# The last turn of a gated layer's second down product: two weight pieces taken row block by row block, and two weight splits moved among the norm's blocks

## The chip, the cores and the metric

The kernel runs on one core of a Trainium2 chip. The metric is the device time of one execution in microseconds (us). The time before is 3171.87 us, the median of 3 runs (3171.06 to 3172.69). Engines are named as in the profile: PE (TensorE, matrix products; PEld its weight loads), DVE (VectorE), ACT (ScalarE), POOL (GpSimd) and SP (SyncE, which issues most DMAs).

## The reference, cut to what matters

The program computes two networks one after the other on 512 tokens of width 1024: first two layers with a gated convolutional feed-forward block, then two layers of another kind. All is float32. The change touches only the feed-forward blocks of the first two layers, and what follows each directly.

```python
D_MODEL = 1024; SEQ = 512; D_FF = 2816
def _conv_ffn(u, w_up, conv_w, conv_b, w_down):
    h = _causal_dwconv(u @ w_up, conv_w, conv_b)
    a, g = jnp.split(h, 2, axis=-1)
    return (jax.nn.gelu(g, approximate=False) * a) @ w_down

    # in first_block, for layer i of 2
        u = x * (1.0 + sc2) + sh2
        y = _conv_ffn(u, f_w_up[i], f_conv_w[i], f_conv_b[i], f_w_down[i])
        x = _layer_norm(DEEPNORM_ALPHA * x + (1.0 + g2) * y, ln_g[i, 1], ln_b[i, 1])
```

After layer 0 comes the attention mixer of layer 1 (`u @ w_in`, in the kernel `d_qk` and `d_v`). After layer 1 comes the second network: an RMS norm, a modulation, and the RWKV time mix, whose first products are small low-rank ones (`sigmoid(xg @ g1)`, `tanh(xw @ w1)`, `xa @ a1`) and then `xr @ wr`.

## The kernel before

**Products in split precision.** Each float32 weight tile is split into a high part (ACT, `act_split`, a copy to a rounded type, `w_high`) and a low part (DVE, `dve_split`, the difference, `w_low`). The left or right operand is split likewise (`u_high`, `u_low`). One product is three PE matmuls (`product`): high by high, high by low, low by high.

**Linears, turns and pieces.** A `Linear` is done in turns of 512 output columns. A turn of a "t" linear fills four PSUM banks, one for each block t of 128 tokens (TT is 4). Its weight comes in pieces of some 128-row steps. `f0_dn1` and `f1_dn1`, the second halves of the two layers' down products, have 10 steps in four pieces of 2, 3, 2 and 3 steps, and two turns. In this text pieces are counted from 0, so the last two are pieces 2 and 3. With four row blocks and three matmuls a piece of 2 steps is 24 matmuls and a piece of 3 steps is 36.

**The ring.** Weight tiles of all linears are numbered through and go through a ring of three slots (`SLOTS`). SP loads tile w once PE has used tile w-3, ACT and DVE split it two tiles ahead of PE (`AHEAD`). So in the last turn of `f0_dn1` the splits that ACT and DVE do "ahead" of pieces 0 and 1 are those of pieces 2 and 3, and those ahead of pieces 2 and 3 are of the next linear's first two tiles. These two are called **next0** and **next1** here. They are tiles of 128 x 2048 elements (1 MB). After `f0_dn1` the next linear is `d_qk`, after `f1_dn1` it is `r_r`. next0 takes the slot of piece 1, next1 that of piece 2, and the tile after them that of piece 3.

**Order.** There is no scheduler. The order on each engine is that in which its program is written, and every engine works strictly in that order. In the last turn `act_residual` does three splits (pieces 2 and 3, next0), then the norm step `follow(0)`, then the split of next1, then `follow(1)` to `follow(3)`. `dve_residual` does the split of piece 2, a block of the modulation (`dve_ada`), the splits of piece 3 and of next0 (all by `dve_ahead_all`), then for each row block t a **block** of the residual and norm, and after all four the split of next1. A block begins with `stage<-bank` (the sum times its gate), then the addition to x, the statistics, and in layer 0 the small operations of `dve_ln_behind`, in layer 1 the longer ones of `dve_r_behind` (two of 128 x 1024). On ACT, `follow(t)` takes a square root, then the normalisation of row block t-1 (and of t too, when t is 3). That row block then goes to PE for transposes (`pe_turn_late`), whose results ACT reads out of PSUM (`act_turn`; after layer 1 the first loop of `act_rwkv`) and DVE works on (`dve_turn`; after layer 1 `dve_rwkv`).

SP's order behind next1 is, after layer 0, two modulation tiles of 1 MB (`ada_ring`) and the next weight tile; after layer 1 the three low-rank weights and two more weight tiles.

Of the kernel before, what the change touches and what calls it, by code (L numbers as in the profile page):

```python
# [14 lines left out]
P = 128  # L15
# [3 lines left out]
TT = S // P  # L19
# [14 lines left out]
DECAY = math.exp(-0.5)  # L34
ROWS = 640
SLOTS = 3
AHEAD = 2
D_UNITS = 32
X_UNITS = 64
# [190 lines left out]
class Net:  # L230
# [499 lines left out]
    def pe_linear_t(self, pe, name, x, ends, u=None, hidden=None, between=None, beside=None):  # L730
        L = self.lin[name]
        for i in range(L.turns):
            for q, (k0, nk) in enumerate(L.pieces):
                w = L.tile(i, q)
                final = q == len(L.pieces) - 1
                if beside and final and i == L.turns - 1:
                    beside()
# [20 lines left out]
                self.pe_ada(pe, L.ada[i])  # L758
            if between and i == 0:
                between()  # L760

    def pe_ada(self, pe, b):
        bank = self.ada_bank.get(b, 7)
# [97 lines left out]
    def dve_residual(self, v, name, st, gates, alpha, lnst=None, follow=None):  # L861
        L = self.lin[name]
        v.wait_ge(self.gates_in, st)
        for i in range(L.turns):
            self.dve_ahead_all(v, name, i)
            for t in range(TT):
                xs, tmp = self.X[:, t, i * 512:(i + 1) * 512], self.stage[:, t % 2, :]
                if t == TT - 1 and i < len(L.ada):
                    self.dve_ada_take(v, L.ada[i])
                v.wait_ge(self.T, "sum", name, i, t)  # L870
                v.wait_ge(self.V)
                v.tensor_tensor(tmp, self.sums(name, i, t)[:], gates[:, i * 512:(i + 1) * 512], ALU.mult).then_inc(
                    *self.V.up("got", name, i, t))
                v.wait_ge(self.V)
                if alpha == 1.0:
                    v.tensor_tensor(xs, xs, tmp, ALU.add).then_inc(*self.V.up("x", name, i, t))
                else:
                    v.scalar_tensor_tensor(xs, xs, alpha, tmp, ALU.mult, ALU.add).then_inc(*self.V.up("x", name, i, t))
                if lnst is not None:
                    v.wait_ge(self.V)  # L880
                    v.bn_stats(lnst[:, t, i * 6:(i + 1) * 6], xs).then_inc(*self.V.up())
                if follow and i == L.turns - 1:
                    follow(t)
            self.dve_ahead(v, name, i, len(L.pieces) - 1)

    def act_residual(self, a, name, follow=None, first=None):
        L = self.lin[name]
        for i in range(L.turns):
            self.act_ahead_all(a, name, i)
            late = follow and i == L.turns - 1  # L890
            if not late:
                self.act_ahead(a, name, i, len(L.pieces) - 1)
            for t in range(TT):
                if first and i == 0:
                    first(t)
                if late:
                    follow(t)
                    if t == 0:
                        self.act_ahead(a, name, i, len(L.pieces) - 1)


# [2200 lines left out]
```

## Time and profile before

| what | value |
|---|---|
| time, median of 3 runs | 3171.87 us |
| profiled execution, its own time | 3168.98 us |
| its span | 3167.70 us |
| PE busy | 2987.9 us, 94% |
| PE weight loads busy | 2433.8 us, 77% |
| DVE busy | 2023.9 us, 64% |
| ACT busy | 1096.4 us, 35% |
| POOL busy | 91.1 us, 3% |
| mean granted PE clock | 0.977 |

The times are taken from one profiled execution and counted from the start of its span; the execution lasted 1.28 us more than the span. PE is busy for nearly all of the span, so what matters is where PE stands still. Two such places, around 748 to 760 us and 1443 to 1468 us, follow the two products that the change touches. A "granted clock" of 1.00 is 2.4 GHz and of 0.50 is 1.2 GHz.

### The profile page before, as it was taken

The numbers are of one execution on the slowest core, as the hardware profiler recorded it, in microseconds if no ns is written. First come the engines' busy times: TensorE is split into PE (matmuls) and PEld (weight loads), VectorE is DVE, ScalarE is ACT, GpSimd is POOL, SyncE is SP. The second block draws the span as 40 slices with busy tenths as digits, with TensorE's granted clock in tenths as the row PEclk, the third lists the DMA queues.
The fourth block names the chain that finished last, engine by engine and source line by source line (L and its number), as shares of the span: only waits on it lengthen the run. The fifth ranks groups of instructions, "written<-read, shape, count | busy, mean of one in ns | idle before, by whom it ended". The sixth has DMA issues, their size and how long they took to land.

```text
span 3167.7 us, 45905 instructions
## 1 busy us (share of the span) xinstructions
PE 2987.9 (94%) x19656; PEld 2433.8 (77%) x19656; DVE 2023.9 (64%) x3115; ACT 1096.4 (35%) x1675; POOL 91.1 (3%) x100
## 2 busy tenths in 40 slices
PE   6998999999988999997999988899999999899999
PEld 5876788887866788884868777678888777778887
DVE  5856897787577896887357888654444255554353
ACT  2334432233155432323333333342223344542122
POOL 0000000000000000000002221000000001000000
PEclk8999999999999999998999999899999999999999
DMA  8751554545620554541310000333323220032232
GB/s 240 182 160 56 184 173 163 182 161 171 201 94 26 174 183 143 205 160 55 108 39 9 12 13 10 103 88 105 93 93 95 80 93 27 8 107 93 94 106 80
DMA packets 236543, 346.08 MB, mean 109 GB/s; under 512 B 19620, under 2 KB 121964, under 8 KB 236340
## 3 DMA queue, kind: packets, MB, share of 16 engines
q1 hardware_dynamic: 221236, 329.63, 32.4%
q10 hardware_dynamic: 15104, 13.52, 1.4%
q8 instruction: 154, 2.52, 0.3%
q14 instruction: 49, 0.40, 0.0%
HBM read 340.97 MB, written 2.15 MB: 108 GB/s over the span
## 4 chain that ended last, share of the span: by engine, by line
PE 79%; DVE 13%; ACT 4%; DMA 2%; issue 1%; SPq 0%; DVEq 0%; ACTq 0%
PE bank L141 77%; DVE w_tiles_b L150 2%; PE bank L144 2%; DVE w_tiles L150 1%; DVE w_low L150 1%; DMA first_ada<-in_w_ada 1%; ACT w_high L147 1%; DVE ada_acc L162 1%; DMA weight_ring<-in_d_w_in 1%; DVE w_g L150 1%; DVE x_natural L162 1%; DVE d_sm L168 0%; ACT stage L147 0%; DVE x_sm L168 0%; DVE x_natural L150 0%
## 5 line engine op out<-in xcount | busy, mean ns | idle before, releaser
L150 DVE TENSOR_TENSOR w_low<-weight_ring,w_high 128x2048 fp32r<-128x2048 f32 (+2 forms) x212 | 463.7, 2187 | 449.3 <-ACT w_high L147 449.3
L147 ACT ACTIVATE w_high<-weight_ring 128x2048 fp32r<-128x2048 f32 (+2 forms) x212 | 388.1, 1831 | 606.6 <-DMA weight_ring<-in_mlp_down 177.7
L141 PE MATMUL bank<-u_high,w_high 128*128 128x512 f32 x1472 | 577.2, 392 | 12.6 <-ACT u_high L147 6.4
L141 PE MATMUL bank<-u_high,w_low 128*128 128x512 f32 x1472 | 573.9, 390 | 0.0
L141 PE MATMUL bank<-u_low,w_high 128*128 128x512 f32 x1472 | 573.5, 390 | 0.0
L141 PE MATMUL bank<-w_high,u_high 128*128 128x512 f32 x896 | 353.5, 395 | 6.2 <-DVE w_low L150 2.5
L141 PE MATMUL bank<-w_high,u_low 128*128 128x512 f32 x896 | 351.4, 392 | 0.0
L141 PE MATMUL bank<-w_low,u_high 128*128 128x512 f32 x896 | 351.2, 392 | 0.0
L141 PEld LDWEIGHTS bank<-u_high,w_high 128*128 128x128 f32 x1472 | 276.9, 188 | 70.8 <-ACT stage L147 7.5
L141 PEld LDWEIGHTS bank<-u_high,w_low 128*128 128x128 f32 x1472 | 276.7, 188 | 58.5
L141 PEld LDWEIGHTS bank<-u_low,w_high 128*128 128x128 f32 x1472 | 277.0, 188 | 56.7
L162 DVE SCALAR_TENSOR_TENSOR ada_acc<-ada_ring,silu_c,ada_acc 128x512 f32<-128x512 f32 x336 | 252.6, 752 | 15.7 <-DVE ada_acc L162 0.5
L141 PEld LDWEIGHTS bank<-w_high,u_high 128*128 128x128 f32 x896 | 170.1, 190 | 45.0 <-DVE w_low L150 2.9
L141 PE MATMUL bank<-w_high,g_hidden_low 128*128 128x512 f32 x512 | 199.2, 389 | 0.0
L141 PE MATMUL bank<-w_high,g_hidden_high 128*128 128x512 f32 x512 | 199.2, 389 | 0.0
L141 PE MATMUL bank<-w_low,g_hidden_high 128*128 128x512 f32 x512 | 199.2, 389 | 0.0
L141 PEld LDWEIGHTS bank<-w_high,u_low 128*128 128x128 f32 x896 | 169.6, 189 | 36.0
L141 PEld LDWEIGHTS bank<-w_low,u_high 128*128 128x128 f32 x896 | 169.9, 190 | 35.1
L150 DVE TENSOR_TENSOR g_relu<-g_relu 128x512 f32<-128x512 f32 x64 | 44.3, 692 | 154.0 <-ACT g_relu L147 154.0
L141 PE MATMUL bank<-w_high,f_hidden_high 128*128 128x512 f32 x352 | 138.0, 392 | 0.0
L141 PE MATMUL bank<-w_high,f_hidden_low 128*128 128x512 f32 x352 | 137.1, 389 | 0.0
L141 PE MATMUL bank<-w_low,f_hidden_high 128*128 128x512 f32 x352 | 137.0, 389 | 0.0
(416 smaller groups left out, 4403.6 us busy)
## 6 DMA issues: line engine op xcount, KB each, us to landing
ada_ring<-in_mod_w SPq DMA_DIRECT2D x48, 1024.0 KB, 7.5
weight_ring<-in_f_w_up SPq DMA_DIRECT2D x44, 1024.0 KB, 5.1
ada_ring<-in_w_ada SPq DMA_DIRECT2D x40, 1024.0 KB, 7.1
weight_ring<-in_mlp_up SPq DMA_DIRECT2D x32, 1024.0 KB, 5.4
weight_ring<-in_mlp_down SPq DMA_DIRECT2D x32, 1024.0 KB, 5.0
weight_ring<-in_f_w_down SPq DMA_DIRECT2D x24, 768.0 KB, 4.7
weight_ring<-in_m_w_in SPq DMA_DIRECT2D x16, 1024.0 KB, 9.7
weight_ring<-in_d_w_in SPq DMA_DIRECT2D x12, 1024.0 KB, 5.1
```

The costliest lines, as they stand in the source:

```text
L141: return self.e.matmul(out, l, r, start=start, stop=stop, skip_group_check=True)
L144: return self.e.transpose(out, in_, ident) if self.live else QUIET
L147: return self.e.activation(out, in_, f, **kw) if self.live else QUIET
L150: return self.e.tensor_tensor(out, a, b, op) if self.live else QUIET
L162: return self.e.scalar_tensor_tensor(out=out, in0=a, scalar=s, in1=b, op0=op0, op1=op1)
```

## The change

In the last turn of `f0_dn1` and `f1_dn1` only:

- PE does pieces 2 and 3 together: for row block 0 the 6 matmuls of piece 2 and the 9 of piece 3, then the same for row blocks 1, 2 and 3. Before, it did piece 2 for all row blocks, then piece 3 for all. The two pieces are marked as used together, with the last row block's sum.
- The split of next0 moves: on ACT from ahead of `follow(0)` to behind `follow(1)`, on DVE from ahead of block 0 to ahead of block 2.
- The split of next1 moves on ACT from behind `follow(0)` to behind `follow(3)`. On DVE it stays behind block 3.

```diff
+BY_ROWS = ("f0_dn1", "f1_dn1")
@@ pe_linear_t
+                if name in BY_ROWS and i == L.turns - 1 and q >= len(L.pieces) - 2:
+                    if q == len(L.pieces) - 2:
+                        self.pe_by_rows(pe, L, x, i)
+                    continue
@@
+    def pe_by_rows(self, pe, L, x, i):
+        for t in range(TT):
+            for q, (k0, nk) in list(enumerate(L.pieces))[-2:]:
+                w = L.tile(i, q)
+                pe.wait_ge(self.V, "split", w)
+                for j in range(nk):
+                    m = self.product(pe, self.bank[L.group(i) + t][:], [y[:, k0 + j, t * P:(t + 1) * P] for y in x],
+                                     [y[:, w % SLOTS, j * 512:(j + 1) * 512] for y in (self.whigh, self.wlow)],
+                                     False, q == len(L.pieces) - 1 and j == nk - 1)
+            m.then_inc(*self.T.up("sum", L.name, i, t))
+            self.free[L.group(i) + t] = (self.V, "got", L.name, i, t)
+        for q in range(len(L.pieces) - 2, len(L.pieces)):
+            self.T.mark("used", L.tile(i, q))
@@ dve_residual
-            self.dve_ahead_all(v, name, i)
+            rows = name in BY_ROWS and i == L.turns - 1
+            if rows:
+                self.dve_ahead(v, name, i, 0)
+                self.dve_ada(v, L.ada[i])
+                self.dve_ahead(v, name, i, 1)
+            else:
+                self.dve_ahead_all(v, name, i)
             for t in range(TT):
+                if rows and t == 2:
+                    self.dve_ahead(v, name, i, 2)
@@ act_residual
-            self.act_ahead_all(a, name, i)
+            rows = name in BY_ROWS and i == L.turns - 1
+            if rows:
+                self.act_ahead(a, name, i, 0)
+                self.act_ahead(a, name, i, 1)
+            else:
+                self.act_ahead_all(a, name, i)
@@
                     follow(t)
-                    if t == 0:
+                    if rows and t == 1:
+                        self.act_ahead(a, name, i, 2)
+                    if t == (TT - 1 if name in BY_ROWS else 0):
                         self.act_ahead(a, name, i, len(L.pieces) - 1)
```

In the changed file every line behind the first one is one further down, so L150 of before is L151 there.

DVE in the last turn of `f0_dn1`, before. The first row is the split of piece 3, the second that of next0, and each `stage<-bank` begins a block of the norm:

```order
L150 TENSOR_TENSOR w_low<-weight_ring,w_high 128x1536
L150 TENSOR_TENSOR w_low<-weight_ring,w_high 128x2048
L150 TENSOR_TENSOR stage<-bank,f_gate_rows 128x512
L150 TENSOR_TENSOR x_natural<-x_natural,stage 128x512
L180 BN_STATS f_lnst<-x_natural 128x6
L183 BN_AGGR f_lnst<-f_lnst 128x2
L150 TENSOR_TENSOR stage<-bank,f_gate_rows 128x512
L150 TENSOR_TENSOR x_natural<-x_natural,stage 128x512
L180 BN_STATS f_lnst<-x_natural 128x6
L183 BN_AGGR f_lnst<-f_lnst 128x2
L177 RECIPROCAL f_lnst<-f_lnst 128x1
L162 SCALAR_TENSOR_TENSOR f_lnst<-f_lnst 128x1
```

The same place after, from the first block on:

```order
L151 TENSOR_TENSOR stage<-bank,f_gate_rows 128x512
L151 TENSOR_TENSOR x_natural<-x_natural,stage 128x512
L181 BN_STATS f_lnst<-x_natural 128x6
L184 BN_AGGR f_lnst<-f_lnst 128x2
L151 TENSOR_TENSOR stage<-bank,f_gate_rows 128x512
L151 TENSOR_TENSOR x_natural<-x_natural,stage 128x512
L181 BN_STATS f_lnst<-x_natural 128x6
L184 BN_AGGR f_lnst<-f_lnst 128x2
L178 RECIPROCAL f_lnst<-f_lnst 128x1
L163 SCALAR_TENSOR_TENSOR f_lnst<-f_lnst 128x1
L151 TENSOR_TENSOR w_low<-weight_ring,w_high 128x2048
L151 TENSOR_TENSOR stage<-bank,f_gate_rows 128x512
```

The split of next0 has moved behind two blocks. It now stands ahead of block 2.

ACT in the last turn of `f0_dn1` and just after, before. The 128x1536 row is the split of piece 3, the two 128x2048 rows are next0 and next1; `x_natural<-x_natural,f_lnst` normalises a row block:

```order
L147 ACTIVATE w_high<-weight_ring 128x1536
L147 ACTIVATE w_high<-weight_ring 128x2048
L147 ACT_TABLE_LOAD
L147 ACTIVATE f_lnst<-f_lnst,small 128x1
L147 ACTIVATE w_high<-weight_ring 128x2048
L147 ACTIVATE f_lnst<-f_lnst,small 128x1
L147 ACTIVATE x_natural<-x_natural,f_lnst 128x1024
L147 ACTIVATE f_lnst<-f_lnst,small 128x1
L147 ACTIVATE x_natural<-x_natural,f_lnst 128x1024
L147 ACTIVATE f_lnst<-f_lnst,small 128x1
L147 ACTIVATE x_natural<-x_natural,f_lnst 128x1024 x2
L147 ACTIVATE stage<-bank,small 128x512 x2
```

The same place after:

```order
L148 ACTIVATE w_high<-weight_ring 128x1536
L148 ACT_TABLE_LOAD
L148 ACTIVATE f_lnst<-f_lnst,small 128x1 x2
L148 ACTIVATE x_natural<-x_natural,f_lnst 128x1024
L148 ACTIVATE w_high<-weight_ring 128x2048
L148 ACTIVATE f_lnst<-f_lnst,small 128x1
L148 ACTIVATE x_natural<-x_natural,f_lnst 128x1024
L148 ACTIVATE f_lnst<-f_lnst,small 128x1
L148 ACTIVATE x_natural<-x_natural,f_lnst 128x1024 x2
L148 ACTIVATE w_high<-weight_ring 128x2048
L148 ACTIVATE stage<-bank,small 128x512 x2
```

next0 now stands behind the normalisation of row block 0, and next1 behind that of row block 3, ahead of the read-out of the transposes.

ACT at the end of `f1_dn1`, before; `r_xn` are the normalised row blocks 2 and 3, `r_u` is the read-out of the transposes:

```order
L147 ACTIVATE ada_ring,small<-x_natural 128x1024
L147 ACTIVATE small<-small 128x1
L147 ACTIVATE r_xn_112<-x_natural,small 128x1024
L147 ACTIVATE r_xn_113<-x_natural,small 128x1024
L147 ACTIVATE r_u<-bank,modulation_columns,small 128x512 x8
```

And after:

```order
L148 ACTIVATE ada_ring,small<-x_natural 128x1024
L148 ACTIVATE small<-small 128x1
L148 ACTIVATE r_xn_112<-x_natural,small 128x1024
L148 ACTIVATE r_xn_113<-x_natural,small 128x1024
L148 ACTIVATE w_high<-weight_ring 128x2048
L148 ACTIVATE r_u<-bank,modulation_columns,small 128x512 x8
```

The split of next1 stands ahead of the read-out here too. PE's rows are the same in number and shape, since only which weight piece and row block each matmul takes has changed, and SP's rows are the same.

## Rows read from the trace of the kernel before

**Rows 1.** Page, section 4: the chain that ended last, shares by engine

```profile
PE 79%; DVE 13%; ACT 4%; DMA 2%; issue 1%; SPq 0%; DVEq 0%; ACTq 0%
```

**Rows 2.** Chain of waits around the end of f0_dn1: start us, us, what

```profile
733.49 5.04 DMA weight_ring<-in_d_w_in
...
738.55 1.93 ACT w_high L147
...
740.50 2.30 DVE w_low L150
...
742.89 0.70 DVE stage L150
...
759.51 5.49 PE bank L141 x23
```

**Rows 3.** Timeline of PE, same place: start us, us, what; first and last matmul of pieces 2 and 3

```profile
733.29 0.39 PE L141 MATMUL bank<-w_high,f_hidden_high 128*128 128x512 f32 x1
...
746.67 0.39 PE L141 MATMUL bank<-w_high,f_hidden_low 128*128 128x512 f32 x1
```

**Rows 4.** Timeline of DVE, same place

```profile
731.48 1.75 DVE L150 TENSOR_TENSOR w_low<-weight_ring,w_high 128x1536 fp32r<-128x1536 f32 x1
...
745.38 0.69 DVE L150 TENSOR_TENSOR stage<-bank,f_gate_rows 128x512 f32<-128x512 f32 x1
...
748.10 0.69 DVE L150 TENSOR_TENSOR stage<-bank,f_gate_rows 128x512 f32<-128x512 f32 x1
...
753.84 2.28 DVE L150 TENSOR_TENSOR w_low<-weight_ring,w_high 128x2048 fp32r<-128x2048 f32 x1
758.21 0.43 DVE L165 CAST u_high<-stage 128x512 fp32r<-128x512 f32 x1 [2.09 <-ACT stage L147]
```

**Rows 5.** Timeline of ACT, same place

```profile
748.03 1.24 ACT L147 ACTIVATE x_natural<-x_natural,f_lnst 128x1024 f32<-128x1024 f32 x1
...
753.46 2.38 ACT L147 ACTIVATE x_natural<-x_natural,f_lnst 128x1024 f32<-128x1024 f32 x2
```

**Rows 6.** Timeline of ACT at the end of f1_dn1

```profile
1448.32 1.06 ACT L147 ACTIVATE ada_ring<-x_natural 128x1024 f32<-128x1024 f32 x1 [1.75 <-DVE x_natural L162]
...
1449.70 1.13 ACT L147 ACTIVATE r_xn<-x_natural,small 128x1024 f32<-128x1024 f32 x1
...
1460.24 2.17 ACT L147 ACTIVATE r_xn<-x_natural,small 128x1024 f32<-128x1024 f32 x2
```

**Rows 7.** Timeline of DVE at the end of f1_dn1

```profile
1443.18 0.69 DVE L150 TENSOR_TENSOR stage<-bank,f_gate_rows 128x512 f32<-128x512 f32 x1
...
1448.46 0.69 DVE L150 TENSOR_TENSOR stage<-bank,f_gate_rows 128x512 f32<-128x512 f32 x1
...
1465.41 0.48 DVE L174 MEMSET r_tw<- 1x512 f32 x1 [2.69 <-PE bank L144]
```

**Rows 8.** Timeline of PE at the end of f1_dn1 and after it

```profile
1441.66 0.39 PE L141 MATMUL bank<-w_high,f_hidden_low 128*128 128x512 f32 x1
...
1468.16 17.94 PE L141 MATMUL bank<-r_xj,r_g 128*128 128x512 f32 x32 [2.91 <-DVE r_xj L162]
```

**Rows 9.** Stretches: from:to, us, busy (x instructions) of PE, PEld, DVE, ACT, POOL, PEclk, DMA share, GB/s

```profile
751.40:758.30 6.90, 5.52 (x25) 5.12 (x26) 4.50 (x10) 4.08 (x6) 0.00 (x0) 0.51 0.05 15
758.30:759.50 1.20, 0.33 (x3) 0.11 (x2) 1.03 (x2) 1.17 (x3) 0.00 (x0) 1.00 0.00 0
759.50:763.00 3.50, 3.49 (x15) 2.90 (x16) 2.98 (x6) 3.23 (x6) 0.00 (x0) 1.00 0.00 0
1465.30:1468.20 2.90, 0.04 (x1) 0.07 (x1) 2.67 (x6) 2.90 (x6) 0.00 (x0) 1.00 0.00 0
1468.20:1471.60 3.40, 3.40 (x4) 0.54 (x4) 3.30 (x8) 2.62 (x3) 0.00 (x0) 0.51 0.00 0
```

**Rows 10.** DMA issues, 738 to 753 us: count, KB each, median us to landing

```profile
weight_ring<-in_d_w_in SPq DMA_DIRECT2D x2, 1024.0 KB, 5.3
ada_ring<-in_mod_w SPq DMA_DIRECT2D x2, 1024.0 KB, 8.5
```

## The prediction

> **What bounds the kernel now.** I read the page's chain first. PE carries 79% of it and DVE 13% [rows 1], so time is lost or won only where PE stands still. Then I read the chain in order of time at the end of `f0_dn1` [rows 2]. The reader is to see that it leaves PE at 733.49, well before the product ends. It goes through the load of next0 (5.04 us), its split on ACT (1.93) and on DVE (2.30, from 740.50), and only then into block 0 at 742.89. From there DVE works through four blocks without a pause, then come the transposes of the last row blocks, and PE starts `d_qk` at 759.51. So the split of next0 holds up the norm, and that is what the change moves. The timelines of PE, DVE and ACT [rows 3 to 8] give what is needed to lay the new order out, and the stretches [rows 9] the clock.
>
> **PE's new order.** The 60 matmuls of pieces 2 and 3 start from 733.29 to 746.67, one each 0.2268 us [rows 3]. By rows the sums of blocks 0 to 3 are 15 matmuls apart, or 3.40 us. A sum can be used some 0.43 us after its last matmul starts (0.39 for the matmul, the rest an estimate for the signal). That is 736.9, 740.3, 743.7 and 747.1. The last one is where it was. Piece 3 is now wanted after 6 matmuls, at 734.65, and its split ends at 731.48 + 1.75 = 733.23 [rows 4], so PE does not wait. Cost 0. In `f1_dn1` the order is the same, the last matmul starts at 1441.66 [rows 8], and the sums come at 1431.9, 1435.3, 1438.7 and 1442.1.
>
> **Block 2 in layer 0.** A block is 748.10 - 745.38 = 2.72 us [rows 4]. Blocks 0 and 1 start with their sums, at 736.9 and 740.3, instead of 742.89 and 745.38. DVE is then free at about 743.0, but what stands next is the split of next0, which waits for its half on ACT, and that half is queued on ACT behind the normalisation of row block 0. ACT began that 748.03 - 745.38 = 2.65 us after block 1 began [rows 4, 5], because it needs the signal from the end of block 1. Now: 742.95, for 1.24 us, until 744.2. Then next0 on ACT for 1.95 from start to start of the DVE half (740.50 - 738.55, rows 2), so DVE splits from 746.15. Block 2 follows 742.89 - 740.50 = 2.39 us later, at 748.54. Before it began at 748.10. All the head start is spent on a DVE wait of 3.1 us and on the split: block 2 is **0.44 us later**, and so are block 3 and the normalisations.
>
> **next1 in layer 0.** Before, both halves were done in the shade of the blocks and the transposes: DVE's from 753.84 to 756.12, and its first operation on u at 758.21 after a wait of 2.09 us [rows 4]. Now ACT's half stands behind the normalisation of row block 3, which ends at 753.46 + 2.38 + 0.44 = 756.3 [rows 5]. DVE's half starts 1.95 later, at 758.25, lasts 2.28 and ends at 760.5. Queued behind it on DVE is the first operation on u, for which PE waits. 760.5 against 758.21 is **+2.3 us** on the start of `d_qk`, and it contains the 0.44. (The transposes, ended at 758.6, are 0.44 us later and still end before it.) The cover of next1 was the 2.09 us wait and the long run of blocks. Nothing replaces it.
>
> **next1's load.** Its slot is piece 2's, which is now marked used at 747.1 instead of about 739. Before, it landed 5.3 us after its issue with two 1 MB tiles right behind it [rows 10]. So it lands at 752.4, ahead of 756.3. Cost 0. The modulation tiles and the next weight tile land behind it within some 14 us, and PE has two tiles of `d_qk` ahead of it then. Cost 0.
>
> **Layer 1.** A block is 1448.46 - 1443.18 = 5.28 us [rows 7]. Block 0 starts at 1431.9, block 1 at 1437.2. ACT's squares start 1448.32 - 1443.18 = 5.14 after a block's start, and the normalisation 1449.70 - 1448.32 = 1.38 later [rows 6, 7]. For row block 0 that is 1443.7, and with 1.18 for it next0's ACT half starts at 1444.9. DVE's half starts at 1446.8 and block 2 at 1449.2, against 1448.46: **0.74 us later**. The last normalisation ends at 1460.24 + 2.17 + 0.74 = 1463.15 [rows 6]. Then next1 on ACT, on DVE at 1465.1, until 1467.37. The memset that opens `dve_rwkv` was at 1465.41 [rows 7], and PE's first low-rank product follows it. That is **+1.95 us**, which contains the 0.74. The low-rank weights are loaded behind one more megabyte, some 3 us later (a third of the 8.5 of rows 10), and they were there 15 us early. Cost 0.
>
> **The clock.** PE's pause before the product lengthens. Behind layer 1 a pause of 2.9 us (PE 0.04 busy) was followed by 3.40 us at 0.51 [rows 9]. Behind layer 0 the pause was 1.20 - 0.33 = 0.87 us and the product began at 1.00, although most of the transposes ahead of it ran at 0.51 [rows 9]. With the change this pause grows by 2.3 - 0.44 = 1.9 us, to 2.7, from 759.1 to 761.8. It is like the one that was followed by the lower clock. A product of 3.4 us at half the clock costs 1.7 us. Ends: 0, if it stays at 1.00, and 3.4, if the transposes' low clock (from 751.4) simply goes on for twice as long. The nearest row is that of 2.9 us, so I take **+1.7**. Behind layer 1 the low stretch exists already; its pause grows from 2.9 to 4.1 us, and the cost lies between -1.7 (it falls into the pause) and +1.7. I take 0.
>
> **Sum.** 2.3 + 1.95 + 1.7 = 5.95 us, on the profiled execution's 3168.98 (span 3167.70) 3174.9. The median is 2.89 above this execution, and on it the sum gives **3177.8 us**. Every us at these places reaches the end, since the chain leaves PE there and PE is its engine elsewhere.
>
> **Rivals.**
> - *The clock stays up behind layer 0.* 5.95 - 1.7 = 4.25, 3176.1. For it: the pause is a little shorter than the one that was followed by the low clock. Against: PE was at 0.51 shortly before.
> - *The clock costs more*, also behind layer 1 (longer pause) or twice as long behind layer 0. Add 1 to 1.7: 3179.2. For it: all PE work ahead of both products is at 0.51 already.
> - *next1 lands late.* In the trace it landed in 5.3 us and the two tiles behind it in 8.5 [rows 10], as if they went in order. Three of them took 8.5 us; were the four now issued together to land together, that is 4/3 of it, 11.3 us: 758.4 instead of 752.4, and ACT stands 2.1 us behind 756.3 with the read-out of the transposes queued behind it. 5.95 + 2.1 = 8.05, 3179.9. The Trainium skill, "DMA: Bandwidth & Descriptors", section "Queues, rings and completion order", says that DMAs of one queue need not complete in the order of issue. By that rule this rival would be live; the trace leans the other way with its 5.3.
> - *The other side: DVE is not held at block 2.* If next0's ACT half were done by the time DVE is free (743.0 and 1442.5), DVE's half would follow at once. Block 3 would start at 743.0 + 2.39 + 2.72 = 748.1 instead of 750.8, and 1442.5 + 2.39 + 5.28 = 1450.1 instead of 1453.7: 2.7 and 3.6 us earlier. With next1 behind it as above (4.2 us from the last normalisation) the starts come 2.3 - 0.44 - 2.7 = -0.8 and 1.95 - 0.74 - 3.6 = -2.4, in sum -3.2: 3168.7. It decides from where ACT's half starts before 741. Against it: ACT works in order, and the row order puts next0 behind the normalisation of row block 0, which needs the end of block 1.
>
> **How the numbers follow.** Forecast 0.44; clock stays 0.22; clock costs more 0.18; late landing 0.06; not held 0.06; the rest 0.04 for something unseen. 0.2% is 6.3 us, about what a measurement of this kernel can tell from no change. The forecast lies 0.4 us below it, so I count a third of it as slower (0.16), with nearly all of the two dearer rivals (0.22 of 0.24) and some of the rest: slower 0.40. Faster by over 0.2% is only in the rest and the far end of "not held": 0.03. The same: 0.57. The range 3172.8 to 3181.6 leaves out "not held" and the rest, and a tenth more of the two dearer rivals, should they come together. The forecast's own range is 3176.5 to 3179.
>
> **What would show it.** Right: on DVE the first `w_low` 128x2048 after two blocks, with an idle time of about 3 us ahead of it ended by ACT; block 2 at 748.5; the second `w_low` 128x2048 ended at 760.5 and the first cast of u directly behind it; PE idle 2.7 us and `d_qk` at 761.8, in a stretch with a granted clock of 0.5. Behind layer 1 the memset directly behind a `w_low`, at 1467.4 plus the shift of layer 0 (2.3, or 4.0 with the clock). Wrong: if block 2 starts before 747, if ACT's second `w_high` 128x2048 is waiting for its DMA, if PE waits between the matmuls of pieces 2 and 3, or if `d_qk` begins before 759.5.

## The result, and the profile after

The changed kernel took 3180.01 us, the median of 20 runs (3175.01 to 3198.74), against 3172.51 for the kernel before, also of 20 (3166.03 to 3183.44). The ratio is 1.003 with an interval of 1.0021 to 1.004: slower, by 6.7 to 12.7 us, with 7.5 between the medians and 9.9 between the means. The forecast was 3177.8, with 0.57 on "the same".

The page of the profiled execution says more and less than that. It was the longest of the 20 (3198.74 us), with a mean granted clock of 0.967 against 0.977 before:

```profile
span 3197.4 us, 45887 instructions
...
PE 77%; DVE 15%; ACT 4%; DMA 2%; issue 1%; SPq 0%; DVEq 0%; ACTq 0%
```

Its span is 29.7 us above that of before, of which only a few us lie where the change is. So I cut both traces at four marks: the last matmul of `f0_dn1`, the moment ACT reads the first sum of `d_qk`, the last matmul of `f1_dn1`, and the moment ACT reads the first sum of the low-rank products. From mark to mark:

| stretch | before | after | difference |
|---|---|---|---|
| last `f0_dn1` matmul to first `d_qk` matmul | 12.84 | 14.82 | +1.98 |
| last `f0_dn1` matmul to first `d_qk` sum read | 23.36 | 26.80 | +3.44 |
| from there to last `f1_dn1` matmul (not touched) | 671.63 | 674.89 | +3.26 |
| last `f1_dn1` matmul to first low-rank matmul | 26.50 | 28.38 | +1.88 |
| last `f1_dn1` matmul to first low-rank sum read | 44.48 | 46.95 | +2.47 |
| from there to the end (not touched) | 1681.54 | 1701.73 | +20.19 |

The change costs 3.44 + 2.47 = 5.91 us at its two places. Of the rest, 23.5 us lie between and behind them and 0.4 ahead of the first, all in code that both kernels share. Two stretches at half the clock hold most of it: 34.1 us, where the kernel before has 10.3 us at 0.50 (1642.3 to 1652.6), and 17.0 us, where it has none. The extra 24 and 17 us are worth about half, 12 and 8.5 (an estimate). Columns are as in [rows 9], first after, then the same stretches in a second profile of the same changed kernel:

```profile
1652.50:1686.60 34.10, 33.77 (x122) 15.73 (x123) 12.03 (x20) 7.45 (x15) 1.33 (x2) 0.50 0.05 8
2714.00:2731.00 17.00, 16.55 (x71) 13.93 (x71) 6.71 (x22) 5.95 (x19) 1.55 (x2) 0.50 0.00 1
```

```profile
1652.50:1686.60 34.10, 32.96 (x351) 19.39 (x352) 16.61 (x30) 11.45 (x23) 5.61 (x8) 0.86 0.04 9
2714.00:2731.00 17.00, 15.10 (x111) 11.98 (x112) 10.32 (x31) 8.93 (x28) 2.38 (x2) 1.00 0.01 1
```

PE was nearly always busy in both. In both the clock falls at about 1652, where PE does the same products, but in the first execution it stays at 0.50 for 34 us, and does so again for 17 us at 2714; in the second the two stretches have 0.86 and 1.00. A span of one execution is thus no measure of a change of 6 us. The times from mark to start at the two places are, since they repeat to a few hundredths in four profiles of the change (below). The times to the first sum hold the clock as well, and repeat less well.

**Where the change is, layer 0.** The chain of waits at the end of `f0_dn1`, after (start us, us, what); the last matmul of `f0_dn1` is 0.36 us later than before in this trace, which is to be taken off for a comparison:

```profile
744.45 1.91 ACT w_high L148
746.39 2.30 DVE w_low L151
...
748.78 0.70 DVE stage L151
...
755.29 1.23 ACT x_natural L148
756.52 1.81 ACT w_high L148
758.35 2.29 DVE w_low L151
```

In [rows 2] the chain had next0's load, its two halves, block 0, and then ran through the norm. Now next0's split is in it ahead of block 2, and next1's as well, in its last 4 us. The load is out of it. DVE's timeline shows both:

```profile
737.26 0.69 DVE L151 TENSOR_TENSOR stage<-bank,f_gate_rows 128x512 f32<-128x512 f32 x1 [3.37 <-PE bank L142]
...
740.66 0.69 DVE L151 TENSOR_TENSOR stage<-bank,f_gate_rows 128x512 f32<-128x512 f32 x1 [1.01 <-PE bank L142]
...
746.39 2.29 DVE L151 TENSOR_TENSOR w_low<-weight_ring,w_high 128x2048 fp32r<-128x2048 f32 x1 [3.12 <-ACT w_high L148]
748.78 0.69 DVE L151 TENSOR_TENSOR stage<-bank,f_gate_rows 128x512 f32<-128x512 f32 x1
...
758.35 2.29 DVE L151 TENSOR_TENSOR w_low<-weight_ring,w_high 128x2048 fp32r<-128x2048 f32 x1 [3.74 <-ACT w_high L148]
760.56 0.42 DVE L166 CAST u_high<-stage 128x512 fp32r<-128x512 f32 x1
```

Blocks 0 and 1 start with their sums, 6.0 and 5.1 us ahead of before (with the 0.36 taken off). Then DVE stands for 3.12 us, because ACT has next0's half behind the normalisation of row block 0. The wait of 2.09 us that hid next1's split [rows 4] is now a wait for ACT's half of that very split, and the cast of u follows it directly. ACT after:

```profile
743.30 1.24 ACT L148 ACTIVATE x_natural<-x_natural,f_lnst 128x1024 f32<-128x1024 f32 x1
744.45 1.90 ACT L148 ACTIVATE w_high<-weight_ring 128x2048 fp32r<-128x2048 f32 x1
...
754.15 2.37 ACT L148 ACTIVATE x_natural<-x_natural,f_lnst 128x1024 f32<-128x1024 f32 x2
756.42 1.89 ACT L148 ACTIVATE w_high<-weight_ring 128x2048 fp32r<-128x2048 f32 x1
758.22 1.42 ACT L148 ACTIVATE stage<-bank,small 128x512 f32<-128x512 f32 x2
```

The second 128x2048 has no wait in brackets: next1 was there (issued at 747.45, and the quickest of the four loads landed in 5.3 us). PE then starts at half the clock. PE's timeline and the stretches (against [rows 9]):

```profile
761.85 0.76 PE L142 MATMUL bank<-u_high,w_high 128*128 128x512 f32 x1 [2.92 <-DVE u_low L151]
```

```profile
751.30:758.20 6.90, 5.42 (x23) 4.62 (x24) 2.96 (x10) 5.65 (x6) 0.00 (x0) 0.51 1.06 381
758.20:761.60 3.40, 0.73 (x7) 0.49 (x5) 3.22 (x3) 2.08 (x4) 0.00 (x0) 1.00 0.66 208
761.60:765.00 3.40, 3.15 (x8) 2.50 (x9) 2.85 (x6) 3.08 (x5) 0.00 (x0) 0.50 0.00 0
765.00:768.00 3.00, 3.00 (x15) 2.46 (x14) 2.55 (x5) 2.78 (x5) 0.00 (x0) 1.00 0.01 3
```

Before, the product had 1.00 from its start. Now its first 3.15 us run at 0.50 (1.2 GHz), behind a pause of 2.92 us.

**Layer 1.** DVE at the end of `f1_dn1`, after, against [rows 7]:

```profile
1453.71 2.29 DVE L151 TENSOR_TENSOR w_low<-weight_ring,w_high 128x2048 fp32r<-128x2048 f32 x1 [4.31 <-ACT w_high L148]
1456.11 0.69 DVE L151 TENSOR_TENSOR stage<-bank,f_gate_rows 128x512 f32<-128x512 f32 x1
...
1471.90 2.29 DVE L151 TENSOR_TENSOR w_low<-weight_ring,w_high 128x2048 fp32r<-128x2048 f32 x1 [3.71 <-ACT w_high L148]
1474.36 0.48 DVE L175 MEMSET r_tw<- 1x512 f32 x1 [0.16 <-issue]
```

The same picture: held for 4.31 us ahead of block 2, and next1's split directly ahead of the memset that PE's low-rank products wait for.

### The profile page after: what moved, and what is told of

It is laid out like the page before. It is cut to its first block, busy times and chain, and to the rows that moved or that the text cites. A ratio compares the mean times of both kernels' runs of the same rounds, so it can differ in the third digit from the quotient of the medians.

```text
span 3197.4 us, 45887 instructions
## 1 busy us (share of the span) xinstructions
PE 3011.9 (94%) x19638; PEld 2451.3 (77%) x19656; DVE 2024.5 (63%) x3115; ACT 1096.4 (34%) x1675; POOL 91.4 (3%) x100
## 4 chain that ended last, share of the span: by engine, by line
PE 77%; DVE 15%; ACT 4%; DMA 2%; issue 1%; SPq 0%; DVEq 0%; ACTq 0%
PE bank L142 76%; DVE w_tiles_b L151 2%; PE bank L145 2%; DVE w_low L151 2%; DVE ada_acc L163 1%; DVE w_tiles L151 1%; DMA first_ada<-in_w_ada 1%; ACT w_high L148 1%; DVE x_natural L151 1%; DVE x_natural L163 1%; DVE w_g L151 1%; ACT stage L148 1%; DMA weight_ring<-in_d_w_in 1%; DVE f_a L163 0%; ACT L148 0%
## 5 line engine op out<-in xcount | busy, mean ns | idle before, releaser
L151 DVE TENSOR_TENSOR w_low<-weight_ring,w_high 128x2048 fp32r<-128x2048 f32 (+2 forms) x212 | 463.8, 2188 | 448.5 <-ACT w_high L148 448.5
L151 DVE TENSOR_TENSOR g_relu<-g_relu 128x512 f32<-128x512 f32 x64 | 44.3, 692 | 153.9 <-ACT g_relu L148 153.9
```

The costliest lines, as they stand in the source:

```text
L151: return self.e.tensor_tensor(out, a, b, op) if self.live else QUIET
```

## The experiments

Each run (11 or 12 executions) was compared with the kernel before on its own chip (29 or 35 executions). The first four experiments share one chip and one set of executions of before, and so do those of each later group, so ratios within a group are not independent. "Local" is the difference from the profile of before between the marks of the table above: first to the first matmul, then to the first sum read. The profile of before is one execution; how its own two places vary is taken up with the delays below.

**One layer each.** The change in layer 0 only, and in layer 1 only.

```diff
-BY_ROWS = ("f0_dn1", "f1_dn1")
+BY_ROWS = ("f0_dn1",)
```

> Layer 0's half of the change alone (the list of names holds only f0_dn1). My theory: the late split of next1 and the blocks held for next0 cost some 2.0 to 2.3 us before d_qk, and the lower clock behind the longer pause another 1.5 to 1.7: together +3.5 to +4 us at the first sum of d_qk against before, and nothing behind layer 1 beyond what the clock of later stages does. Rival (the extra time of the changed kernel comes from later stages, where the clock falls more often once everything is shifted): the local cost is 3.5 us, but the whole time rises by more than that, because of stages that the edit does not touch.

Measured: 3176.17 against 3170.69, ratio 1.0017 (1.0009 to 1.0026). Local: layer 0 +1.98 and +3.31, layer 1 -0.05 and -0.04.

```diff
+BY_ROWS = ("f1_dn1",)
```

> Layer 1's half of the change alone (the list holds only f1_dn1). My theory: nothing moves up to the end of f1_dn1; the first low-rank product starts 1.95 us later relative to the last sum (the memset behind the split of next1), and the low clock there costs between -1.7 and +1.7 more. Time +2 us over before. Rival: the low stretch behind layer 1 grows each time, then +3.5 us.

Measured: 3174.4 against 3170.69, ratio 1.0014 (1.0003 to 1.0025). Local: layer 0 +0.15, layer 1 +1.88 and +2.46. The two places are independent, and each alone costs what it costs in the pair: 3.31 + 2.46 = 5.8, with 5.9 for both in the first profile. The whole time rose by more, +5.3 and +4.1 us between means.

**next1's split back in the shade of block 3**, next0's left where the change put it:

```diff
-                    if t == (TT - 1 if name in BY_ROWS else 0):
+                    if t == (2 if name in BY_ROWS else 0):
```

> The whole change, but ACT's half of next1 stands between the norm steps of row blocks 2 and 3 (behind follow(2)) instead of behind follow(3). My theory, that the late split of next1 is the larger cost: behind layer 0 its load lands about 752.4, ACT's half delays the last normalisations by some 0.5 to 1 us, and d_qk starts about 1.0 us later than in the changed kernel's case without it, that is +0.7 to +1.2 us against before instead of +2.0; behind layer 1 the split is hidden altogether and the first low-rank product starts +0.74 us against before instead of +1.95. Rival (the cost is the block held for next0, or PE's order): both starts stay where the changed kernel has them, +2.0 and +1.95.

Measured: 3178.85 against 3170.69, ratio 1.0026 (1.0014 to 1.0039). Local: layer 0 +0.83 and +3.04, layer 1 +1.66 and +2.29. The start of `d_qk` gains 1.15 of 1.98 us and the clock takes most of it back by the sum: 2.21 us between start and sum, although PE's pause was only 0.66 us here. The low clock of the transposes simply went on. In layer 1 the expectation failed. DVE there, and ACT beside it:

```profile
1461.19 1.28 DVE L163 SCALAR_TENSOR_TENSOR x_natural<-x_natural,f_lnst,f_ln_g 128x1024 f32<-128x1024 f32 x1
1463.17 0.17 DVE L178 RECIPROCAL f_lnst<-f_lnst 128x1 f32<-128x1 f32 x1 [0.69 <-ACT f_lnst L148]
```

```profile
1461.06 1.90 ACT L148 ACTIVATE w_high<-weight_ring 128x2048 fp32r<-128x2048 f32 x1
1462.86 0.28 ACT L148 ACTIVATE f_lnst<-f_lnst,small 128x1 f32<-128x1 f32 x1
```

ACT had begun the split when block 3 asked it for its square root, and block 3 waited 0.69 us. In layer 0 the reciprocal of row block 3 waits 0.68 us in the same way. At this place ACT's half of next1 takes 1.9 us and delays the norm instead of `u`.

**Both splits placed where nothing waits**: next0's ACT half behind `follow(0)`, next1's two halves behind the reads of the transposes and, in layer 1, behind the first eight mixes.

```diff
-                    if rows and t == 1:
+                    if rows and t == 0:
                         self.act_ahead(a, name, i, 2)
-                    if t == (TT - 1 if name in BY_ROWS else 0):
+                    if t == (99 if name in BY_ROWS else 0):
@@ dve_residual, behind the four blocks
-            self.dve_ahead(v, name, i, len(L.pieces) - 1)
+            if not rows:
+                self.dve_ahead(v, name, i, len(L.pieces) - 1)
@@ act, behind act_turn "d u"
+        self.act_ahead(a, "f0_dn1", 1, 3)
@@ dve, behind dve_turn "d u"
+        self.dve_ahead(v, "f0_dn1", 1, 3)
@@ act_rwkv, behind the reads of r_u
+        self.act_ahead(a, "f1_dn1", 1, 3)
@@ dve_rwkv, behind the first eight mixes
+            if before is None:
+                self.dve_ahead(v, "f1_dn1", 1, 3)
```

> PE's new order kept, both splits placed so that nothing waits for them: next0 on ACT behind follow(0), on DVE ahead of block 2 as in the change; next1 on ACT behind the read-out of the transposes, on DVE behind the work on u (layer 0) or behind the first eight mixes (layer 1). My theory, that PE's order is a gain which the two splits ate: behind layer 0 block 3 starts 2.7 us earlier than before and d_qk some 2.7 us earlier, behind layer 1 the low-rank product 3.6 us earlier, together -5 to -6 us against before, and faster than it. PE may wait up to 0.5 us for next1 in d_qk. Rival (PE's order is worth nothing, the norm's own chain sets the start): within 1 us of before.

Measured: 3163.22 against 3170.69, ratio 0.9976 (0.9965 to 0.9988). Local: -3.88 and -3.91, -3.63 and -3.67. DVE in layer 0 shows the hold gone:

```profile
746.30 2.29 DVE L151 TENSOR_TENSOR w_low<-weight_ring,w_high 128x2048 fp32r<-128x2048 f32 x1
748.70 0.69 DVE L151 TENSOR_TENSOR stage<-bank,f_gate_rows 128x512 f32<-128x512 f32 x1
```

In this trace the last matmul of `f0_dn1` was 3.49 us later than in the trace of before, so block 2 at 748.70 is 748.10 + 3.49 - 748.70 = 2.89 us earlier than in [rows 4]. The other 1.0 of the 3.88 is in the last transposes, which here kept the full clock (chain of waits, and stretches of the same kernel):

```profile
755.50 1.48 PE bank L145 x11
...
759.11 2.97 PE bank L142 x12
```

```profile
753.00:757.00 4.00, 2.24 (x20) 1.94 (x19) 1.41 (x6) 2.60 (x4) 0.00 (x0) 1.00 1.07 382
757.00:758.90 1.90, 0.72 (x7) 0.48 (x5) 1.06 (x2) 1.87 (x3) 0.00 (x0) 1.00 1.07 391
```

Repeated on another chip:

> The version with both splits mended once more, for whether it beats both kernels on another chip. My theory: local -1.6 and -3.8 us against before, as in its first profile, so 3 to 8 us faster than before and 9 to 13 us faster than the changed kernel in the same call. Rival (its 7.5 us were luck of one chip): within 2 us of before.

Measured: 3168.22 against 3176.75, ratio 0.9979 (0.9964 to 0.9994), local -3.88 and -3.89, -3.54 and -2.49. (The expectation gives -1.6 for layer 0 in the first profile; that profile has -3.88.) This version beats the kernel before twice, by 7.5 and 8.5 us, and with it the changed kernel, which in the same comparison as the repeat was 10.6 us slower than it.

**The moved splits without the row order.** PE does pieces 2 and 3 as before:

```diff
-                if name in BY_ROWS and i == L.turns - 1 and q >= len(L.pieces) - 2:
+                if False:
```

> The two splits moved exactly as in the change, but PE in its old order (piece 2 for all row blocks, then piece 3). My theory: without the early sums the held block is dearer. Behind layer 0 the sums come about 740.9 and 743.0, row block 0 is normalised from 746.3, next0 is split on DVE from 749.5, block 2 starts at 751.9 instead of 748.1, and with next1 behind it d_qk starts some 5.4 us later than before. Behind layer 1: block 0 at 1435.8, block 2 at about 1453, some 4.6 us late, and the low-rank product some 5.8 us late. In all +11 us, so PE's order by itself is worth about 7 us. Rival (PE's order is worth nothing): +2 and +2 us locally, as in the changed kernel.

Measured: 3185.67 against 3177.26, ratio 1.0029 (1.0017 to 1.0041). Local: +5.14 and +6.71, +5.95 and +7.25. DVE, layer 0:

```profile
741.45 0.69 DVE L151 TENSOR_TENSOR stage<-bank,f_gate_rows 128x512 f32<-128x512 f32 x1 [7.83 <-PE bank L142]
...
749.66 2.29 DVE L151 TENSOR_TENSOR w_low<-weight_ring,w_high 128x2048 fp32r<-128x2048 f32 x1 [3.11 <-ACT w_high L148]
```

The hold is 3.11 us here too, so it doesn't come from the row order but from where ACT's half stands. (With PE's old order the slot of piece 2 comes free earlier again as well.) The row order itself is worth 5.14 - 1.98 = 3.2 us in layer 0 and 5.95 - 1.88 = 4.1 us in layer 1. The moved splits lose all of it and more.

**next0's ACT half one step earlier**, nothing else:

```diff
-                    if rows and t == 1:
+                    if rows and t == 0:
```

> The whole change, but ACT's half of next0 stands behind follow(0) instead of behind follow(1); next1 stays late, as in the change. My theory: DVE no longer waits 3.1 us at block 2, blocks 2 and 3 start 2.7 us (layer 0) and 3.6 us (layer 1) earlier than before. next1 is then the whole local cost: behind layer 0 it may still land after ACT is free for it, and d_qk starts 0 to 0.8 us earlier than before; behind layer 1 the low-rank product 2.4 us earlier. Local sum -2.4 to -3.2 us. Rival (the late next1 is the whole cost and the hold costs nothing): +1.5 and +1.2 us, little better than the changed kernel.

Measured: 3174.89 against 3177.26, ratio 0.9993 (0.9979 to 1.0008). Local: -1.08 and +0.27, -2.54 and -1.96. DVE, layer 0:

```profile
743.54 2.29 DVE L151 TENSOR_TENSOR w_low<-weight_ring,w_high 128x2048 fp32r<-128x2048 f32 x1
...
755.64 2.29 DVE L151 TENSOR_TENSOR w_low<-weight_ring,w_high 128x2048 fp32r<-128x2048 f32 x1 [3.75 <-ACT w_high L148]
757.85 0.42 DVE L166 CAST u_high<-stage 128x512 fp32r<-128x512 f32 x1
```

This is the mechanism of the prediction's fourth rival, which put the two starts at -0.8 and -2.4. The move of one line takes 3.1 and 4.4 us off the two starts. next1's split still stands ahead of the cast, and the clock still takes 1.35 us between start and sum.

**next0 held, next1 out of the way.** The opposite half: next1 placed as in the version with both mended, next0 as in the change (the edit above without its first pair of lines).

> The whole change, with next0 where the change has it (DVE held at block 2), but next1 moved out of the way (on ACT behind the read-out of the transposes, on DVE behind the work on u or the first eight mixes). This leaves the hold alone. My theory: block 2 starts 0.44 us late behind layer 0 and 0.74 us late behind layer 1, and so do d_qk and the low-rank product; with the clock up to 1.7 us more in each. Rival (the hold costs nothing by itself): both starts as before, or earlier.

Measured: 3177.89 against 3176.75, ratio 1.0004 (0.9992 to 1.0015). Local: +0.32 and +0.29, +0.88 and +0.88. DVE, layer 0:

```profile
745.46 2.29 DVE L151 TENSOR_TENSOR w_low<-weight_ring,w_high 128x2048 fp32r<-128x2048 f32 x1 [3.12 <-ACT w_high L148]
...
757.98 0.43 DVE L166 CAST u_high<-stage 128x512 fp32r<-128x512 f32 x1 [4.29 <-ACT stage L148]
```

So the hold at block 2 makes up 0.3 and 0.9 of the two start delays against before, and next1's place the other 1.7 and 1.0. Against the version with both mended the hold costs much more, 4.2 and 4.5 us: it eats the head start.

**PE's pause filled.** The change, with 8 bf16 matmuls of a constant into an unused bank ahead of `d_qk`, and 10 ahead of the low-rank products:

```diff
+        self.pe_keep(pe, self.turn_bank("d u", 0), 8)
         self.pe_linear_f(pe, "d_qk", "d u",
@@ pe_rwkv, behind the transposes
+        self.pe_keep(pe, self.turn_bank("r", 0), 10)
```

> The whole change, and PE does 8 small products that nobody reads in its pause before d_qk and 10 in its pause before the low-rank products. My theory, that a lower clock behind the longer pause is 1.5 us of the cost in layer 0: the stretch of d_qk's first products is at 1.00, d_qk's first sum is read 1.5 us sooner than in the changed kernel's profile, that is +2.0 us against before instead of +3.5, and the low stretch of 3.4 us behind layer 1 is gone (up to 1.7 us). The whole time falls by 1.5 to 3 us against the changed kernel. Rival (the clock costs nothing that matters, or the fill is itself in the way): the first sum stays at +3.5, or later where the fill runs at the low clock.

Measured: 3171.61 against 3177.26, ratio 0.9992 (0.9979 to 1.0004). Local: +1.90 and +1.98, +1.87 and +0.22. PE's timeline and stretches in layer 0 (the trace has seven of the eight filler matmuls):

```profile
760.37 2.37 PE L142 MATMUL bank<-core_constants 128*128 128x512 bf16 x7 [0.22 <-ACT stage L148]
762.39 0.58 PE L142 MATMUL bank<-u_high,w_high 128*128 128x512 f32 x1
```

```profile
751.50:761.70 10.20, 8.09 (x32) 6.35 (x34) 6.01 (x16) 7.82 (x9) 0.00 (x0) 0.50 0.98 342
761.70:765.00 3.30, 3.30 (x16) 2.51 (x15) 2.77 (x5) 2.56 (x4) 0.00 (x0) 0.99 0.00 0
```

The start is as late as in the change, but the product has 0.99 from its beginning. The part of the clock in layer 0, 3.44 - 1.98 = 1.46 us, is gone. In layer 1 the sum even gains 1.65 on the start, since there the kernel before had the low stretch too [rows 9]. In all 17 profiles, 23 products at these two places stand behind a pause of 2.3 to 4.2 us, and each of them began at 0.50 or fell to it within 0.3 us (one, in layer 1 of the kernel with next0 held, after 1.2 us); the two behind a filled pause had 0.99 and 1.00. So what the change adds at the clock in layer 0 comes with the pause. The filled kernel is 5.2 us below the changed one in the mean on the same chip, more than the 3.0 us that it gains at the two places; the other 2 us are not explained.

A long pause is not the only way to a slow start of `d_qk`. After the short pauses of 0.66 to 1.4 us there, seven profiles have 1.00 and two have 0.50, both with a pause of 0.66 us: the one with next1 earlier, and one of the kernel before with a delay far ahead of it (4.3 us, below), whose transposes and product are those of before. (The pause is the shortest of all there because the slow transposes end later: their last 18 take 4.10 us, against 3.88 in the profile of before.)

```profile
762.71 0.77 PE L141 MATMUL bank<-u_high,w_high 128*128 128x512 f32 x1 [0.66 <-ACT u_high L147]
```

```profile
753.10:762.70 9.60, 6.83 (x29) 5.58 (x29) 6.92 (x16) 6.13 (x9) 0.00 (x0) 0.50 0.21 67
762.70:766.80 4.10, 4.09 (x10) 3.23 (x11) 3.59 (x6) 3.79 (x7) 0.00 (x0) 0.50 0.02 4
```

There the first sum came 1.93 us later than in the profile of before, with the start at +0.00. The kernel before thus pays this price itself in one of the five profiles that show its layer 0.

**The change again, on three chips**, and delays of known length put into the kernel before (12, 20 and 28 of the same filler matmuls ahead of `f0_dn1`), to see what a known delay does to the whole and how the kernel before's own two places vary:

> The changed kernel once more. Its profile shows two long stretches at the low clock, at 1652 to 1687 and at 2714 to 2731 us, in stages that the change does not touch, worth some 11 and 9 us. My theory: they are chance of the one execution and are absent here; the span is near 3178 and the local costs are +3.5 (plus or minus 1.7 from the clock) and +2.1 us as in the first profile. Rival (the change brings them about, by when the later stages start): they are here again, and the span is over 3190.

> The changed kernel against the kernel before a third time. The first comparison gave 1.0030 and the second 1.0003, and their intervals do not meet, while the two profiles give nearly the same local cost (5.5 and 5.2 us). My theory: the local cost is all there is and both comparisons were pulled by which chip and which executions they got; this one gives +3 to +8 us, a ratio of 1.0010 to 1.0025. Rival (the change costs some 9 us through the later stages): 1.0028 or more again.

> The changed kernel against the kernel before a fourth time. The three comparisons so far gave 1.0030, 1.0003 and 1.0004, and the kernel before had means of 3172.5, 3177.1 and 3177.0 us in them. My theory: the change costs its local 5.5 us, and what differs is how much the kernel before loses at the clock on the chip in question. If its mean is near 3172 here the ratio is 1.0025 or more, if it is near 3177 it is 1.0003 to 1.0017. Rival (plain scatter, no tie to the kernel before's own level): the ratio does not follow that level.

```diff
+        if l == 0:
+            self.pe_keep(pe, self.lin["f0_dn1"].group(0), 12)
         self.pe_linear_t(pe, st + "_dn1", f["hid"], self.V, hidden=st + "_up1")
```

> The kernel before with nothing but a delay: PE does 12 products that nobody reads ahead of f0_dn1, 12 x 0.213 = 2.6 us in a place where PE is never waited out. The question is whether a shift of the whole rest costs just its own length. My theory: it does, +2.6 us, give or take the scatter of single executions. Rival (the low-clock stretches sit at nearly fixed times, so that a shift makes later pauses fall into them or out of them): the whole time rises by 2 to 4 us more, or less, than the delay.

> As the delay of 12, with 20 products, 4.3 us. My theory: +4.3 us. Rival (shift of later stages against the clock): differs from the delay by 2 to 4 us, and not by the same amount as with 12 and 28.

> As the delay of 12, with 28 products, 6.0 us, about what the change costs locally. My theory: +6.0 us. Rival (shift of later stages against the clock): +8 to +10 us, as the first comparison of the changed kernel showed, because the later stages come to lie as they do there.

| kernel | local (to the sum), layer 0 / 1 | this / before, medians | ratio (interval) | difference of means |
|---|---|---|---|---|
| change, first | +3.44 / +2.47 | 3180.01 / 3172.51 | 1.003 (1.0021 to 1.004) | +9.9 |
| change, second | +3.48 / +1.76 | 3179.55 / 3177.26 | 1.0003 (0.9992 to 1.0014) | +1.8 |
| change, third | +3.57 / +1.77 | 3177.5 / 3177.83 | 1.0004 (0.9991 to 1.0016) | +1.9 |
| change, fourth | +3.32 / +2.21 | 3178.8 / 3176.75 | 1.0017 (1.0003 to 1.0032) | +4.6 |
| delay of 2.6 us | +0.19 / +1.08 | 3179.81 / 3177.83 | 1.0009 (0.9998 to 1.002) | +3.1 |
| delay of 4.3 us | +1.93 / +0.77 | 3177.19 / 3177.83 | 1.0006 (0.9992 to 1.002) | +2.6 |
| delay of 6.0 us | +0.00 / +1.33 | 3180.9 / 3177.83 | 1.0019 (1.0007 to 1.0031) | +5.1 |

Against the one profile of before the local cost is the same to some tenths in four profiles: 5.9, 5.2, 5.3 and 5.5 us. But the delays, which touch neither place, show local differences of their own, 1.3, 2.7 and 1.3 us, mostly from the clock: the profile of before was a favourable one. With the mean of the five profiles that show the kernel before's code at each place, and the five that show the change's, the cost is 3.0 us in layer 0 and 1.5 in layer 1, 4.5 in all.

The total differs more: +9.9, +1.8, +1.9 and +4.6 us, on average 4.5. The third lies below what was expected of it (1.0010 to 1.0025). The delays cost 0.6 to 1.2 times their length, which shows no multiplier behind them, but the intervals are wide: that of the longest is 2.2 to 9.9 us for 6.0. Both kernels move between comparisons. The mean of before was 3172.5 in the first and 3171.4 with the first four experiments, but 3177.0 to 3177.1 in the others; that of the changed kernel was 3182.4, 3179.0, 3179.0 and 3181.7. So of the 8 us by which the first difference exceeds the second and third, some 4.5 lie in before and 3.4 in the changed kernel. Take the thirteen comparisons of kernels with an edit at the two places: where the mean of before was 3171 to 3173, all five differences of means exceed the local figure, by 0.6 to 3.9 us; where it was 3177, seven of eight fall short of it, by 0.3 to 5.6. So the ratio of one comparison hangs on the level that before happens to have in it. Why the level depends on the chip or the hour, the runs do not tell.

## Why the prediction was right and wrong

- **PE's new order: right.** Blocks 0 and 1 started at 736.90 and 740.30 on the clock of before, as forecast, and PE had no wait for piece 3.
- **Block 2: right.** A DVE wait of 3.12 us for ACT (forecast 3.1). Block 2 came 0.32 us later than before instead of 0.44. In layer 1 the wait was 4.31 us and block 2 came 0.59 us later (forecast 0.74).
- **next1: right, a little dear.** Its DVE half ended at 760.3 on the clock of before (forecast 760.5), with the cast directly behind it. `d_qk` started +1.98 late, not +2.3; the low-rank product +1.88, not +1.95.
- **next1's load: right.** ACT's half waited for no DMA. The rival of the late landing did not occur, in spite of four loads on the way at once; the two weight tiles and the two modulation tiles had a median of 8.6 us each, but the one that was needed first came in 5.3.
- **The clock: right in kind, a little dear.** Layer 0: 2.9 to 3.4 us of the product at 0.50, worth 1.34 to 1.59 us in the four profiles (forecast 1.7). Layer 1: between -0.1 and +0.6 (forecast 0, ends -1.7 and 1.7). The filled pause shows that the pause brings it. Two things the prediction didn't see: in the fourth profile the low stretch of the transposes never ended before the product (it runs from 753.0 to 766.6), which was the prediction's other end, at 1.34 us and not 3.4; and the 1.00 of before, on which the whole +1.7 rests, is not certain, since before had 0.50 there in one of five profiles.
- **The rival on the other side** named the hold as what decides. Taking the hold away gave -1.08 and -2.54 at the starts (-0.8 and -2.4 worked out), so the price was right and so was the reason why it would not occur.
- **The sum: right at its places.** 5.95 forecast, 5.2 to 5.9 measured against the same profile of before, each time a little below. Against the mean of five profiles of before it is 4.5, so by that measure the sum was some 1.5 us dear, over half of it in the clock.
- **How the numbers follow: this step failed.** The first comparison is +6.7 to +12.7 us, on the side "slower by over 0.2%", on which I had put 0.40, while 0.57 stood on "the same". The mechanism at the two places held; what failed is the step from the sum to the chances. I had set a local sum of 5.95 against a limit of 6.3 us and counted only a third of the forecast as slower (a third of 0.44 is 0.15, not 0.16), as if what stood between sum and measured time were a few tenths. Three runs of before within 1.6 us had led me to that. In 20 runs the kernel before spans 17 us, the changed one 24, and the mean of before differs by up to 5.7 us between comparisons. Beside a sum of 5.95 such a spread leaves "same" and "slower" nearly even. In the three further comparisons (1.0003, 1.0004, 1.0017) the ratio stays below 0.2%, so which side came out was in part luck, and so would a hit have been. Whether the 4 us by which the means of the first exceed the local cost belong to the change in any way stays open: what its trace shows beyond the local cost are the two long stretches at 0.50. The first came again, just as long, in the profile of the fourth comparison and in no other, the second in that of the 4.3 us delay, which has nothing of the change, and the delays show no multiplier. That points away from the change, but doesn't show it.

## What to carry to other kernels

A split of two halves on two in-order engines stands where its slower queue lets it. Before moving one among other work, ask what stands ahead of each half: here ACT's half, behind a normalisation, held DVE for 3.1 us and ate a head start of 5 us that PE's new order had won. And whatever is moved out of a shade must land in another: the same two splits, with ACT's half of next0 one step earlier and next1 behind the last read that PE waits for, turned a local +5.5 us into -6.4 to -7.6.

When a forecast lies near the limit of what can be told, the sum at the place is checked by the trace, but the whole time is a draw from a distribution. Take the chances from the spread of many executions, not from three. And the trace at the place needs a baseline of several executions too: one profile of before made the change look 1 us dearer than five did.

## What the runs showed of the hardware

- In the four profiles of the change PE's pause ahead of `d_qk` was 2.3 to 2.9 us, and 2.9 to 3.4 us of the product ran at 0.50, where a pause of 0.9 us had been followed by 1.00 [rows 9]. Eight bf16 matmuls in the pause (PE idle 0.22 us ahead of them) left the product at 0.99, although the stretch that they stood in was itself at 0.50.
- After a pause of 0.66 us `d_qk` started at 0.50 in two profiles, where the transposes ahead of it had been at 0.50 to their end; after pauses of 0.77 to 1.4 us it started at 1.00 in seven.
- PE can be held at 0.50 while it is busy: 34.1 us with PE busy for 33.77, and 17 us with 16.55, in one execution of a program of which another execution had 0.86 and 1.00 there. At the place of the first, two thirds of PE's time is in the products `r_g2a` and `r_g2b`, and 14 of the 17 profiles have a stretch at 0.50 of 7 to 14 us there, two have the 34 us, and one has none. The Trainium skill, "TensorE: Matmul & The Clock Gate", section "What's actually happening", ties the clock to how busy PE has lately been; the trace of this place shows it low with PE busy, and no run here shows what makes it last.
- Of four 1 MB loads issued behind one another the first landed in 5.3 us, the median was 8.6 and the last took 12.0.
